# Modulation chunks moved behind the norms' roots, and rests of expert weights in another order

## The reference, cut to what matters

```python
mod = jax.nn.silu(c) @ w_mod[layer] + b_mod[layer]      # six vectors of 1024, for c and for c_ctx
sh_t, sc_t, gt_t, sh_f, sc_f, gt_f = split(mod, 6)
a = rms_norm(h, g_pre_t) * (1 + sc_t) + sh_t            # goes into the mixer
h = h + gt_t * rms_norm(mixer(a), g_post_t)
...
a, g = jnp.split(xb @ w13[e], 2, axis=-1)               # one block of 128 rows, one expert
out = (jax.nn.silu(a) * g) @ w2[e]
```

## Time and profile before

| | us |
|---|---|
| median of 3 runs | 2451.89 |
| lowest and highest | 2443.71, 2451.92 |
| the profiled execution | 2443.37 |
| its span, first to last instruction | 2441.3 |

### The profile page before, as it was taken

How to read it: one execution, slowest core, us unless ns; L and a number is a source line. 1 busy time by engine, 2 the same in 40 slices (tenths; PEclk the granted TensorE clock), 3 DMA queues, 4 the chain that set the end, 5 groups by cost and what they waited for, 6 DMA issues and landing times.

```text
span 2441.3 us, 33170 instructions
## 1 busy us (share of the span) xinstructions
PE 2344.0 (96%) x12602; PEld 1922.7 (79%) x12602; DVE 1700.6 (70%) x1797; ACT 1355.5 (56%) x1442; POOL 46.0 (2%) x89
## 2 busy tenths in 40 slices
PE   6999999998999998998997999999999999999998
PEld 4867778876788886868986888888888888888887
DVE  4867644426333336797658888898989898888886
ACT  3455442334222233656456777777777777777774
POOL 0010000001000000010000000000000000000000
PEclk9999999999999999999998999999999999999999
DMA  7243123345422233443656999999999999999893
GB/s 284 95 139 126 61 96 111 104 165 218 135 95 95 96 103 122 164 160 114 204 190 240 364 349 366 345 367 348 365 349 363 348 366 351 363 343 371 342 372 134
DMA packets 103251, 569.05 MB, mean 233 GB/s; under 512 B 11760, under 2 KB 13680, under 8 KB 54640
## 3 DMA queue, kind: packets, MB, share of 16 engines
q1 hardware_dynamic: 91632, 525.72, 57.9%
q0 software_dynamic: 11520, 41.95, 4.8%
HBM read 566.58 MB, written 1.05 MB: 233 GB/s over the span
## 4 chain that ended last, share of the span: by engine, by line
PE 88%; DVE 5%; ACT 3%; issue 1%; SPq 1%; DMA 1%; DVEq 0%; ACTq 0%
PE bank L662 27%; PE bank L664 26%; PE bank L663 26%; PE bank L858 1%; PE bank L880 1%; PE bank L1107 1%; PE bank L1175 1%; PE bank L753 1%; DVE hres L1671 1%; PE bank L867 1%; DMA mod_s<-in_mod 1%; PE bank L721 1%; DVE cacc L1696 1%; DVE wlo L1612 1%; DVE y L1668 1%
## 5 line engine op out<-in xcount | busy, mean ns | idle before, releaser
L1945 DVE TENSOR_TENSOR elo<-eraw,ehi 128x2048 fp32r<-128x2048 f32 x378 | 862.4, 2288 | 132.1 <-ACT ehi L1279 131.1
L1279 ACT CAST ehi<-eraw 128x2048 fp32r<-128x2048 f32 x378 | 722.3, 1914 | 246.5 <-PE bank L664 239.7
L1612 DVE TENSOR_TENSOR wlo<-raw,whi 128x1024 fp32r<-128x1024 f32 x220 | 269.2, 1224 | 238.7 <-ACT whi L1227 237.2
L662 PE MATMUL bank<-ah,whi 128*128 128x512 f32 (+1 forms) x1088 | 395.6, 364 | 9.8 <-DVE wlo L1612 5.8
L662 PE MATMUL bank<-ehi,xgh 128*128 128x512 f32 x1016 | 402.0, 396 | 2.1 <-DVE xgl L1951 1.7
L664 PE MATMUL bank<-ehi,xgl 128*128 128x512 f32 x1016 | 396.6, 390 | 0.0
L663 PE MATMUL bank<-elo,xgh 128*128 128x512 f32 x1016 | 395.8, 390 | 0.0
L663 PE MATMUL bank<-al,whi 128*128 128x512 f32 (+1 forms) x1088 | 389.6, 358 | 0.0
L664 PE MATMUL bank<-ah,wlo 128*128 128x512 f32 (+1 forms) x1088 | 389.3, 358 | 0.0
L1227 ACT CAST whi<-raw 128x1024 fp32r<-128x1024 f32 x220 | 229.0, 1042 | 109.0 <-PE bank L664 108.8
L662 PEld LDWEIGHTS bank<-ah,whi 128*128 128x128 f32 x1088 | 207.6, 191 | 45.0 <-issue 8.4
(11 more groups left out here) (268 smaller groups left out, 2656.0 us busy)
## 6 DMA issues: line engine op xcount, KB each, us to landing
eraw<-in_moe SPq DMA_DIRECT2D x378, 1024.0 KB, 4.9
raw<-in_dense SPq DMA_DIRECT2D x220, 512.0 KB, 3.3
mod_a<-in_mod POOLq DMA_DIRECT2D x40, 512.0 KB, 3.6
mod_b<-in_mod POOLq DMA_DIRECT2D x40, 512.0 KB, 7.2
mod_s<-in_mod SPq DMA_DIRECT2D x16, 512.0 KB, 13.3
hres<-in_xT SPq DMA_DIRECT2D x1, 2048.0 KB, 7.7
wsT<-in_wsT SPq DMA_DIRECT2D x2, 512.0 KB, 3.5
out_h<-hres SPq DMA_DIRECT2D x2, 512.0 KB, 2.9
```

What stands on the lines that cost most here:

```text
L662: pe.matmul(dst, wh, xh, start=first, stop=False, skip_group_check=True)
L1279: nc.scalar.copy(ehi[c % ESPLIT][:], eraw[c % ERAW][:]).then_inc(e_hi, 1)
L1612: dve.tensor_tensor(wlo[c % SPLIT][:], raw[c % RAW][:], whi[c % SPLIT][:].bitcast(F32), ALU.subtract).then_inc(w_lo, 1)
L1945: dve.tensor_tensor(elo[c % ESPLIT][:], eraw[c % ERAW][:], ehi[c % ESPLIT][:].bitcast(F32), ALU.subtract).then_inc(e_lo, 1)
```

## The change

Four edits.

1. In the two norms (layer 0 ahead of the SwiGLU, and layer 1's entrance) the last three chunks of the second vector leave their places between the squares and go behind the roots and the first vector's turn. The second vector's `copy_rows` goes behind `affine_hi`, and its `turn_rows` behind the column pair. VectorE's order isn't touched.
2. In attention's step 1 two modulation chunks run, and none in step 2.
3. At the expert loop's entrance the casts of chunks 2 and 3 go ahead of the copies of the turned tokens; the rest of chunk 1 goes ahead of the top two, the rest of chunk 2 behind them, the rest of chunk 3 behind the slots.
4. In each block, VectorE's rests of chunks 10 and 11 go behind `hTl` and the three additions of the scatter step.

```diff
+MOD_HELD = 3
...
+        def mods_in_step(s):
+
+            return {1: 2, 2: 0}.get(s, 1)
...
-                        mod_chunk()
+                        if k < KD - MOD_HELD:
+                            mod_chunk()
                     n.next(sumsq_psum)
                     spread_roots(TOK)
                     turn_rows(MOD_ATT_1 - 2)
-                    turn_rows(MOD_ATT_1 - 1)
+
+                    for _ in range(MOD_HELD):
+                        mod_chunk()
...
                     column_pair((("kv0", L), ("kv1", L)), ah, al, xw, TOK)
+                    turn_rows(MOD_ATT_1 - 1)
...
                                 column_pair((("fa", 0), ("fg", 0)), ah, al, xw, TOK)
+                                turn_rows(MOD_GAP + 1)
...
                     copy_rows(MOD_GAP)
+                    affine_hi(1, TOK, ah)
                     copy_rows(MOD_GAP + 1)
-                    affine_hi(1, TOK, ah)
...
+            for c in range(2, 4):
+                round_e(0, c)
             for t in range(2):
                 for half in range(2):
                     act.wait_ge(ft_psum, 2 * t + half + 1)
...
             rest_e(0, 0)
+            rest_e(0, 1)
             dve.wait_ge(lg_psum, 1)
...
+            rest_e(0, 2)
+
             dve.wait_ge(rank_psum, 1)
...
             slots_of(rr, slice(0, 1))
-            rest_e(0, 1)
+            rest_e(0, 3)
             rest_gathered(0)
-            rest_e(0, 2)
...
             of_blocks(rrp[:], rr16[:])
-            rest_e(0, 3)
             rest_e(0, 4)
...
                     if kind == "scatter":
                         add_rows(it, half)
+                        if not half:
+
+                            for p in range(2):
+                                rest_next(it, EPRE + ESPLIT + p, steps)
...
-                    elif kind in ("a", "g"):
+                    elif (kind, q) != ("a", 1) and kind in ("a", "g"):
                         rest_next(it, c + ESPLIT, steps)
```

More of the change, by code:

```diff
@@ L919, in _ @@
                     if s < len(MOD_ATT[L]) * KD:
-                        mod_chunk()
+                        for _ in range(mods_in_step(s)):
+                            mod_chunk()
                 for i in range(4):
@@ L1038, in _ @@
                     turn_rows(MOD_GAP)
-                    turn_rows(MOD_GAP + 1)
+                    for _ in range(MOD_HELD):
+                        mod_chunk()
                 else:
@@ L1304, in _ @@
                     copy_rows(MOD_ATT_1 - 2)
+                    affine_hi(0, TOK, ah)
                     copy_rows(MOD_ATT_1 - 1)
-                    affine_hi(0, TOK, ah)
                 def low_rank(t, name, ntok):
@@ L1539, in _ @@
             nc.scalar.activation(ew[:, 2:4], ew[:, 0:2], ACT.Exp).then_inc(e_exp, 1)
-            for c in range(2, 4):
-                round_e(0, c)
             copy_gathered(0)
```

## The result

| | before | changed |
|---|---|---|
| median of 20 runs each, us | 2446.58 | 2464.8 |
| lowest and highest | 2440.13, 2456.45 | 2454.49, 2468.19 |
| profiled execution, us | 2443.37 | 2465.54 |
| its span, us | 2441.3 | 2463.4 |

The account below looks back on a forecast made before the run. TensorE was taken as the bound nearly everywhere. Terms 1.9 + 2.9 - 0.3 - 0.5 - 3.2 + 8.3 = +9.1 us, on the three-run median 2451.89, gave 2461 us (+0.37%), range 2447 to 2467.

Parts of the forecast that it names:

- the sum's bad end: Whole kernel: the bad ends of the terms, +15 us on the upper level 2451.9, gave the range's top, 2467.
- Waits of the norms: Dense norm and layer 1's entrance: the next tile waits for a rest queued behind modulation; +1.9 and +2.9 us.
- Rival D: Both norms: VectorE isn't held by the turn, so 1.9 and 2.9 go; 2448 with a free loop; chance 0.03.
- The pairs: Column pairs of both norms: chunks moved into the gap ahead; -0.3 us taken, -2.0 if the clock stays up.
- the case against: Norms: against the clock staying up stood that squares without chunks run at 0.50.
- Attention: Layer 0's attention: a chunk moves into the wait for the first exponential; -0.5 us, between -3 and 0; layer 1: 0.
- Entrance: Expert loop's entrance: stall of 6.46 us becomes 0.9, then a 3.6 us wait for `hTl`; -3.2 us net.
- Loop: Eight further blocks: TensorE waits for the second `hTl`, 1.04 us per block; +8.3 us, bounds +5 to +11.
- Rival A: Expert loop: its new order costs nothing; +0.8 us in all, 2452.7; chance 0.14.
- Rival C: Expert loop: later fetches of chunk 16 delay every block, paid nine times; at 10.4 us +27, 2479; chance 0.08.
- Rival B: Clock stays up at all four places: pairs -2.0, attention -3, entrance -5.6; +2.5 us in all, 2454.4; chance 0.09.

Follow-up runs that it names:

- before, again: The kernel before, unchanged, profiled once more; its span was 2447.3 us.
- edit 3 with one rest of 4: Kernel before plus the entrance's earlier casts and rests, and only chunk 11's rest moved behind the additions; ratio 0.9966, and again 0.9970 (-7.3 us).
- The turn alone: Kernel before with only the second turn put behind the pair in both norms, all chunks in their old places; ratio 1.0020 (+4.9 us).
- edit 4 alone: Kernel before with only the rests of chunks 10 and 11 moved behind the scatter's additions in every block; ratio 1.0031 (+7.6 us).

## Why the prediction was right or wrong

The time, 2464.8, lies in the range 2447 to 2467, near its upper end; the forecast, 2461.0, is 3.8 below. As a change it was forecast at +9.1 us and is +14.4. By its own bound of half a per cent, the likeliest case (within 0.5%, 0.74) is not what came: 0.59% is just beyond it, though the interval still touches 0.47%.

- **The base.** The forecast was counted from the median of three runs, 2451.89. Over 20 runs it is 2446.58. That made the absolute forecast 5.3 us too high and hid as much of what the sum lacked. That the time lies inside the range is in part luck: the sum's bad end was +15, which from 2446.58 is 2461.6, below the measured median.
- **Waits of the norms: right.** 1.9 and 2.9 were forecast. In the changed kernel the tile stands 2.50 us behind the pair's end instead of 0.66, +1.84, and 986.37 - 983.36 = 3.01 instead of 0.25, +2.76. VectorE's idle time ahead of `modT`, released by the turn, is there twice. Rival D is out.
- **The pairs: wrong sign.** -0.3 was taken between -2 and +2; the pairs end 0.77 and 0.21 later. What the step gave as the case against came about, save for the place: the clock fell at 566.2, behind the last squares, which still ran at full clock; in the changed kernel's second profile it fell among the squares. The roots took 2.08 instead of 1.16 and the chunks 2.79. But the clock costs time up to and into the pair without the edit too (+1.34 in before, again, +2.16 in edit 3 with one rest of 4), so how much of the 0.77 is the edit's can't be told.
- **What failed: the clock behind the norms' waits was no term of the sum.** It cost 4.18 - 0.77 - 1.84 = 1.57 and 4.34 - 0.21 - 2.76 = 1.37 us. The prediction had said that 1.84 and 2.25 us of idle time suffice for a fall, and priced that at the entrance, where it was about to forecast a gain, but not in the norms. The turn alone had the same waits without it, so it is a risk with a price of about 1.5 each, not a certainty; what decides it stays open.
- **Attention: -0.5 forecast, -0.13 found,** and 0 in layer 1 as forecast. The step took TensorE to be the path from the first exponential on. The next one was late as well.
- **Entrance: right, and nearly in size.** -3.2 was forecast, -3.9 came. The fourth chunk ended 1.2 earlier (1.1 forecast), the wait for `macc` is 0.87 (0.9), that for `hTl` 3.44 (3.6), and up to this `w2` the gain is 5.6 as worked out. The fall of the clock behind it cost 1.7 where 2.4 was taken (2.6 in edit 4 alone).
- **Loop: right.** +8.3 forecast, +8.84 found. The chain was put at 22.5 us and is 22.53; the wait is 0.85, the restart 0.3 instead of 0.1, so 1.16 per block and not 1.04 (about 0.8 in the last of the eight). Rival A is out, by edit 4 alone as well. Rival C is out: ScalarE waits in the loop only for TensorE, with no row for `eraw`. The fetches did get slower, as C feared: the median from issue to landing rose from 4.9 to 6.6 us, still inside the 8.4 that the step counted for it.
- **Rival B,** the clock stays up: at the four places of the changed kernel it fell, so its +2.5 did not come. The Trainium skill, TensorE: Matmul & The Clock Gate, section "What's actually happening", says that activity releases the throttle. The -2.0 that was put beside this rule did not come: the three chunks in the gap ran at 0.50 themselves (569 to 572), and the clock was back half a microsecond into the pair.

Put together: 9.1, and 2.9 for the clock behind the norms' waits, 1.3 for the pairs, 0.4 for attention, 0.5 for the loop, less 0.7 for the entrance and 0.2 for the two waits is 13.3, which the stretches measured add up to.

## What to carry to other kernels

Before work is moved into an idle slot, see who waits for its result and what is queued behind that wait on the same engine: here a rest needed by the next tile stood behind a modulation that nobody needed yet, and moving one instruction ahead of the wait, in each norm, took the measured loss away. In a loop, count one engine's instructions between two meetings with the bounding engine before anything is moved inside: one rest of 2.2 us behind the additions was free, two cost 1.1 us in each of eight blocks. A count tells when the chain becomes the bound (22.5 counted, 22.53 measured), and not how much is to spare below that, where the engine waits for others (1.3 counted, 0.4 measured). And profile the kernel before twice, since one profile of it does not tell which of its half-clock stretches belong to the program.

## What the runs showed of the hardware

The granted clock behind a wait is no function of the waits alone. In attention of layer 1, waits equal to 0.01 us were followed by 1.00 throughout in one execution of a program and by 0.50 over 12 us in another, 5.7 us apart at the end. In layer 0 the same place cost 0, 1.6 or 3.2 us in the profiles where nothing was changed there. Between such steps two profiles of the same code agreed to some hundredths of a microsecond over hundreds, the whole loop to 0.01 us in 967. So a single pair of profiles can mislead by 6 us in either direction on this kernel, while differences taken stretch by stretch are good to 0.05 us, at the expert entrance to 0.2, once these steps are set apart.
